# Feed-forward phase of a decoder layer: gate and up products from seven block products, gated values through memory, down product by token quarters

## The chip, the core and the metric

One core of one Trainium2 chip runs the whole layer as one program. The metric is the device time of one execution in microseconds (us). The change touches the last phase of the program only, the feed-forward part.

## The reference

The layer takes x (1 x 2048 x 1024, float32), mixes tokens with two kinds of sparse attention, and ends with a gated feed-forward network and a layer norm. The part that matters here:

```python
h = layer_norm(ALPHA * x + mixed @ w_out, ln1_g, ln1_b)        # 2048 x 1024
ffn = (jax.nn.silu(h @ w_gate) * (h @ w_up)) @ w_down          # w_gate, w_up: 1024 x 2816, w_down: 2816 x 1024
return layer_norm(ALPHA * h + ffn, ln2_g, ln2_b)
```

## The kernel before

The program is a row of phases with a barrier between them: projection, compression, attention, mixing (which writes h and its transpose h_t to memory) and `ffn_phase`. Every float32 product is made as three products of values in the fp32r form: each operand is split into a high part, which ScalarE rounds (`high`), and a low part, which VectorE subtracts (`low`); TensorE then adds high x high, high x low and low x high in one PSUM bank. Each is one instruction of 128 rows, 128 columns of weights and 512 moving columns.

The 2048 tokens are taken in four groups of 512 (`over_groups`: the groups 0, 1 and 3 are written out, group 2 is the body of a loop). In each group:

- **Gate and up** (`gate_up`). For each of the 22 blocks of 128 hidden columns (`f`) SyncE loads 128 columns of `w_gate` and of `w_up` (1024 x 128, 512 KB each) into `raw[0]` and `raw[1]`; ScalarE and VectorE split them into `w_hi` and `w_lo`; TensorE makes 8 x 3 products for gate and 8 x 3 for up, each in one bank. ScalarE makes silu of gate, VectorE multiplies it by up (`prod`), and the product is split again into `g_hi` and `g_lo`, which hold all 22 blocks on chip.
- **Down** (`for d in range(2 * DOWN)`). The 1024 output columns are taken in two halves of 512; in each half 11 steps bring two blocks of `w_down` rows (512 KB), and each step makes 2 blocks x 4 token tiles x 3 = 24 products into the four banks `acc[0..3]`. At the end of a half VectorE adds ALPHA x h from `y` (`after`, line 2280), and the next half may overwrite a bank only after that. The x operand of the next group is loaded between steps (`X_AFTER`).
- **Norm.** VectorE takes the moments, GpSimd the root of the variance, ScalarE normalizes, GpSimd multiplies by the gain and adds the offset (lines 2118 and 2121). For groups 0 to 2 this lies in the gate and up stage of the next group.

The order on every engine is the order of the program; engines wait for each other by counting semaphores. The two slots of `raw`, `w_hi` and `w_lo` are used in turn: a slot is loaded again after its low part is made, and split again after the product that read it (`used`). SyncE issues every transfer of the phase, in order.

Of the kernel before, what the change touches and what calls it, by code (L numbers as in the profile page):

```python
# [1940 lines left out]
GROUP = 512  # L1941
N_GROUPS = SEQ // GROUP
FT = FFN // P
DOWN = FT // 2


def ffn_phase(nc, h, h_t, w_gate, w_up, w_down, ln_g, ln_b, out):
# [4 lines left out]

    NB = GROUP // P
    HALF = D_MODEL // 2
    W_PER = 2 * FT + 2 * DOWN
    NX = KT * GROUP // D_MODEL
    X_AFTER = {2: 0, 6: 1, 13: 2, 17: 3}
    S_PER = W_PER + NX

    def raw_of_down(d, last):  # L1960

        return d if last else d + sum(1 for k in X_AFTER if k < d)

    with ExitStack() as ctx:  # L1964
# [6 lines left out]
        def psum(name, cols):  # L1971
            return ctx.enter_context(nc.psum_tensor(name, [P, cols], F32))

        raw = sb("f_raw", [P, 2, D_MODEL])
        w_hi = sb("f_w_hi", [P, 2, D_MODEL], F32R)
        w_lo = sb("f_w_lo", [P, 2, D_MODEL], F32R)
        x_hi = sb("f_x_hi", [P, KT, GROUP], F32R)
        x_lo = sb("f_x_lo", [P, KT, GROUP], F32R)
        silu = sb("f_silu", [P, 2, GROUP])
        prod = sb("f_prod", [P, 2, GROUP])  # L1980
        g_hi = sb("f_g_hi", [P, FT, GROUP], F32R)
        g_lo = sb("f_g_lo", [P, FT, GROUP], F32R)
        y = sb("f_y", [P, NB, D_MODEL])
        g_b = sb("f_ln_g", [P, D_MODEL])
        b_b = sb("f_ln_b", [P, D_MODEL])
# [8 lines left out]
        gate_ps = [psum(f"f_gate{b}", GROUP) for b in range(2)]  # L1994
        up_ps = [psum(f"f_up{b}", GROUP) for b in range(2)]
        acc = [psum(f"f_acc{b}", HALF) for b in range(NB)]

        small_ld = sem("f_small_ld")
        raw_ld = [sem(f"f_raw_ld{b}") for b in range(2)]
        y_ld = sem("f_y_ld")  # L2000
        hi_done = sem("f_hi_done")
        lo_done = sem("f_lo_done")
        used = sem("f_used")
        silu_done = sem("f_silu_done")
        prod_done = sem("f_prod_done")
        g_hi_done = sem("f_g_hi_done")
        g_lo_done = sem("f_g_lo_done")
# [12 lines left out]
        gate_cols = w_gate.rearrange("(k p) n -> p k n", p=P)  # L2020
        up_cols = w_up.rearrange("(k p) n -> p k n", p=P)
        down_rows = w_down.rearrange("(f p) n -> p f n", p=P)
        xt_rows = h_t.rearrange("(k p) n -> p k n", p=P)
        h_rows = h.rearrange("(g t p) n -> g p t n", p=P, t=NB)
        out_rows = out.rearrange("(g t p) n -> g p t n", p=P, t=NB)

        def over_groups(eng, body):

            body(0, True, False)
            body(1, False, False)  # L2030
            with eng.Fori(2, N_GROUPS - 1) as g:
                body(g, False, False)
            body(N_GROUPS - 1, False, True)

        @block.sync
        def _(sp):
            def load(s, parity, src, shape=None):

                if not isinstance(s, int) or s >= 2:
                    sp.wait_ge(lo_done, s - 1)  # L2040
                dst = raw[:, parity]
                if shape:
                    dst = dst.rearrange("p (a n) -> p a n", a=shape)
                sp.dma_start(dst, src).then_inc(raw_ld[parity], 16)

            def load_x(s, parity, g, n):
                load(s, parity, xt_rows[:, 2 * n:2 * n + 2, bass.ds(g * GROUP, GROUP)], 2)

            for dst, src in ((g_b, ln_g.broadcast_to([P, D_MODEL])), (b_b, ln_b.broadcast_to([P, D_MODEL]))):
                sp.dma_start(dst[:, :], src).then_inc(small_ld, 16)  # L2050
            for n in range(NX):
                load_x(n, n % 2, 0, n)

            def store(g):

                sp.wait_ge(y_done, NB * (g + 1))
                sp.dma_start(out_rows[bass.ds(g, 1), :, :, :].rearrange("o p t n -> (o p) t n"), y[:, :, :]).then_inc(y_out, 16)

            def body(g, first, last):
                s0 = NX + g * S_PER  # L2060
                with sp.Fori(0, FT) as f:
                    for m, cols in enumerate((gate_cols, up_cols)):
                        load(s0 + 2 * f + m, m, cols[:, :, bass.ds(f * P, P)], KT)

                if not first:
                    store(g - 1)
                    sp.wait_ge(y_out, 16 * g)
                sp.dma_start(y[:, :, :], h_rows[bass.ds(g, 1), :, :, :].rearrange("o p t n -> (o p) t n")).then_inc(y_ld, 16)
                for d in range(2 * DOWN):
                    s = raw_of_down(d, last)  # L2070
                    half, b = divmod(d, DOWN)
                    load(s0 + 2 * FT + s, s % 2, down_rows[:, 2 * b:2 * b + 2, half * HALF:(half + 1) * HALF], 2)
                    if d in X_AFTER and not last:
                        load_x(s0 + 2 * FT + s + 1, (s + 1) % 2, g + 1, X_AFTER[d])

            over_groups(sp, body)
            for t in range(NB):
                sp.wait_ge(y_done, NB * (N_GROUPS - 1) + t + 1)
                sp.dma_start(out_rows[N_GROUPS - 1, :, t, :], y[:, t]).then_inc(y_out, 16)
            sp.wait_ge(y_out, 16 * (N_GROUPS - 1 + NB))  # L2080

        def down_splits(split, split_x, g, last, after):

            for d in range(2 * DOWN):
                e = d + 2
                if e - 1 in X_AFTER and not last:
                    split_x(NX + g * S_PER + 2 * FT + raw_of_down(e, last) - 1, (raw_of_down(e, last) - 1) % 2, X_AFTER[e - 1], g)
                if e < 2 * DOWN:
                    split(NX + g * S_PER + 2 * FT + raw_of_down(e, last), raw_of_down(e, last) % 2, g * W_PER + 2 * FT + e, e % 2)
                elif not last:  # L2090
                    m = e - 2 * DOWN
                    split(NX + (g + 1) * S_PER + m, m, (g + 1) * W_PER + m, m)
                after(d)

        def raw_landed(eng, s, parity):
            eng.wait_ge(raw_ld[parity], (s - parity + 2) * 8)

        @block.gpsimd
        def _(pool):
            for c, value in ((power, -0.5), (eps, LN_EPS), (minus, -1.0)):  # L2100
                pool.memset(c[:, :], value).then_inc(fixed_set, 1)
            pool.wait_ge(fixed_set, 3)
            pool.wait_ge(small_ld, 32)

            def body(g, first, last):
                n0 = g * NB
                for t in range(NB):
                    pool.wait_ge(aggr_done, n0 + t + 1)
                    pool.tensor_tensor(rstd[:, t:t + 1], aggr[:, t, 1:2], eps[:, :], ALU.add).then_inc(rstd_done, 1)  # L2109
                    pool.tensor_tensor(nmr[:, t:t + 1], aggr[:, t, 0:1], minus[:, :], ALU.mult).then_inc(rstd_done, 1)  # L2110
                    pool.wait_ge(rstd_done, 4 * (n0 + t) + 2)
                    pool.tensor_tensor(rstd[:, t:t + 1], rstd[:, t:t + 1], power[:, :], ALU.pow).then_inc(rstd_done, 1)
                    pool.wait_ge(rstd_done, 4 * (n0 + t) + 3)
                    pool.tensor_tensor(nmr[:, t:t + 1], nmr[:, t:t + 1], rstd[:, t:t + 1], ALU.mult).then_inc(rstd_done, 1)
                for t in range(NB):
                    pool.wait_ge(normed, n0 + t + 1)
                    if not last:
                        pool.tensor_tensor(y[:, t], y[:, t], g_b[:, :], ALU.mult).then_inc(gained, 1)

                    pool.wait_ge(gained, n0 + t + 1)  # L2120
                    pool.tensor_tensor(y[:, t], y[:, t], b_b[:, :], ALU.add).then_inc(y_done, 1)  # L2121

            over_groups(pool, body)

        @block.tensor
        def _(pe):
            def product(out, a, w, start, stop):
                return pe.matmul(out, a, w, start=start, stop=stop)  # L2128

            def body(g, first, last):  # L2130
                s0, w0 = NX + g * S_PER, g * W_PER

                def gate_up(f, q, wait_bank):
                    for m, ps in enumerate((gate_ps, up_ps)):
                        pe.wait_ge(lo_done, s0 + 2 * f + m + 1)
                        if wait_bank:

                            pe.wait_ge(prod_done, g * FT + f - 1)
# [219 lines left out]
```

## Time and profile before

| what | value |
|---|---|
| time of three runs | 4007.77, 4009.16 and 4015.93 us, median 4009.16 |
| profiled execution, its own time | 4008.02 us |
| its span, first to last instruction | 4006.0 us |
| mean granted TensorE clock | 0.945 |
| TensorE busy | 3669.9 us, 92% of the span |
| VectorE, ScalarE, GpSimd busy | 1838.5, 1650.0 and 765.1 us |
| moved by DMA | 273.15 MB, 68 GB/s |

The durations below come from the one profiled execution. Its own time is 2.0 us above its span. A matmul row shows a matmul from issue to its last result; several are in the pipe at once, so the distance between the starts of two of them is what one of them costs in a dense stretch, and not its duration. PEclk is the granted clock as a share of full speed.

### The profile page before, as it was taken

To read this page: it belongs to the slowest core of one execution; us is meant where nothing else is said; L and a number is where in the kernel's file an instruction comes from. 1 tells how busy PE (TensorE), PEld (TensorE's weight loads), DVE (VectorE), ACT (ScalarE), POOL (GpSimd) and SP (SyncE) were. 2 spreads that over 40 slices of the span, in tenths; PEclk is the share of its full clock that TensorE was granted. 3 is DMA by queue.
4 is the path that set the end of the run, shared out by engine and by line. 5 is a ranking of instruction groups with operands and counts; after the bars stand their busy time and mean duration, and the time that the engine had idled before them with its cause. 6 is when DMAs were issued, how large, how long until landed. Compare 5 with 4: busy or idle time off the path is not lost. (4 is left out here: it accounts for less than half of the span.)

```text
span 4006.0 us, 56003 instructions
## 1 busy us (share of the span) xinstructions
PE 3669.9 (92%) x19448; PEld 3110.9 (78%) x19448; DVE 1838.5 (46%) x4296; ACT 1650.0 (41%) x2690; POOL 765.1 (19%) x1650
## 2 busy tenths in 40 slices
PE   6999768989898999999999697999999999999997
PEld 5999647877777788888778585788788788878885
DVE  4222145666666666776664343333343243324323
ACT  2000024667666677677765332232232233223321
POOL 0000023454343333332321132000020020002001
PEclk9999768999999999999889898999999999999998
DMA  4221220000000000000000354333333433433342
GB/s 144 74 69 62 67 50 26 24 16 22 16 9 16 15 16 13 10 7 10 4 6 6 124 158 147 105 94 129 103 94 112 135 100 94 142 109 96 94 136 74
DMA packets 302064, 273.15 MB, mean 68 GB/s; under 512 B 32544, under 2 KB 249760, under 8 KB 299680
## 3 DMA queue, kind: packets, MB, share of 16 engines
q1 hardware_dynamic: 300368, 268.31, 21.8%
q10 hardware_dynamic: 1488, 2.20, 0.2%
q8 instruction: 114, 1.87, 0.2%
q14 instruction: 94, 0.77, 0.1%
HBM read 218.57 MB, written 51.90 MB: 68 GB/s over the span
## 5 line engine op out<-in xcount | busy, mean ns | idle before, releaser
L2224 DVE TENSOR_TENSOR f_w_lo<-f_raw,f_w_hi 128x1024 fp32r<-128x1024 f32 x264 | 337.3, 1278 | 883.7 <-ACT f_w_hi L2176 883.7
L2176 ACT ACTIVATE f_w_hi<-f_raw 128x1024 fp32r<-128x1024 f32 x264 | 279.9, 1060 | 882.6 <-PE f_acc L2128 337.2
L1285 ACT ACTIVATE a_p_t<-a_ps_st 128x512 f32<-128x512 f32 x716 | 438.0, 614 | 371.3 <-PE a_ps_st L1175 191.7
L1292 ACT ACTIVATE a_junk_a<-a_index,a_tk 128x384 bf16<-128x384 f32 (+13 forms) x336 | 445.0, 1325 | 110.3 <-DVE a_halves L1402 55.6
L1201 PEld LDWEIGHTS a_ps_o<-a_vsl,a_p_t 128*128 128x128 f32 x2176 | 315.5, 209 | 26.4 <-DVE a_fin L1499 3.4
L2128 PE MATMUL f_gate<-f_x_hi,f_w_hi 128*128 128x512 f32 x704 | 275.1, 391 | 30.2 <-DVE f_w_lo L2224 30.2
L1201 PE MATMUL a_ps_o<-a_vsl,a_p_t 128*128 128x65 f32 x2176 | 298.2, 284 | 2.1 <-DVE a_fin L1499 2.1
L1201 PEld LDWEIGHTS a_ps_o<-a_dv,a_p_t 128*128 128x128 f32 x2176 | 290.0, 194 | 9.0
L2128 PE MATMUL f_acc<-f_w_hi,f_g_hi 128*128 128x512 f32 x704 | 278.6, 396 | 16.4 <-DVE f_y L2280 12.6
L2128 PE MATMUL f_acc<-f_w_lo,f_g_hi 128*128 128x512 f32 x704 | 277.2, 394 | 0.0
L2128 PE MATMUL f_acc<-f_w_hi,f_g_lo 128*128 128x512 f32 x704 | 277.0, 393 | 0.0
L2128 PE MATMUL f_gate<-f_x_lo,f_w_hi 128*128 128x512 f32 x704 | 274.6, 390 | 0.0
L2128 PE MATMUL f_gate<-f_x_hi,f_w_lo 128*128 128x512 f32 x704 | 274.6, 390 | 0.0
L2109 POOL TENSOR_TENSOR f_rstd<-f_aggr,f_eps 128x1 f32<-128x1 f32 x16 | 6.5, 406 | 1402.1 <-DVE f_aggr L2254 1402.1
L1201 PE MATMUL a_ps_o<-a_dv,a_p_t 128*128 128x65 f32 x2176 | 274.0, 269 | 0.0
L2128 PE MATMUL f_up<-f_x_hi,f_w_hi 128*128 128x512 f32 x704 | 273.9, 389 | 0.0
L2128 PE MATMUL f_up<-f_x_lo,f_w_hi 128*128 128x512 f32 x704 | 273.9, 389 | 0.0
L2128 PE MATMUL f_up<-f_x_hi,f_w_lo 128*128 128x512 f32 x704 | 273.9, 389 | 0.0
L188 PE MATMUL p_acc<-pw_hi,px_hi 128*128 128x448 f32 x640 | 238.5, 373 | 34.2 <-DVE pw_lo L267 33.9
L188 PE MATMUL p_acc<-pw_lo,px_hi 128*128 128x448 f32 x640 | 237.3, 371 | 0.0
L188 PE MATMUL p_acc<-pw_hi,px_lo 128*128 128x448 f32 x640 | 237.3, 371 | 0.0
L1382 DVE SCALAR_TENSOR_TENSOR a_index<-a_relu,a_iw,a_index 128x512 f32<-128x512 f32 (+3 forms) x266 | 179.7, 716 | 99.6 <-ACT a_relu L1279 96.9
(268 smaller groups left out, 7556.7 us busy)
## 6 DMA issues: line engine op xcount, KB each, us to landing
f_raw<-in_w_gate SPq DMA_DIRECT2D x88, 512.0 KB, 3.8
f_raw<-in_w_up SPq DMA_DIRECT2D x88, 512.0 KB, 3.8
f_raw<-in_w_down SPq DMA_DIRECT2D x88, 512.0 KB, 3.3
z_scratch<-p_z SPq DMA_DIRECT2D x16, 1120.0 KB, 5.2
pw_raw<-in_w_in SPq DMA_DIRECT2D x16, 560.0 KB, 3.8
px_raw<-in_x_t SPq DMA_DIRECT2D x16, 512.0 KB, 6.4
o_scratch<-a_oacc SPq DMA_DIRECT2D x32, 256.0 KB, 2.1
m_o_in<-o_scratch SPq DMA_DIRECT2D x16, 512.0 KB, 4.5
```

What stands on the lines that cost most here:

```text
L188: mm = pe.matmul(acc[c][:, 0:CH], xs[:, u, k], ws[:, k, c * CH:(c + 1) * CH], start=(k == 0 and n == 0), stop=last)
L1201: mm = pe.matmul(ps_o[n % 2][:, h * cols:(h + 1) * cols], p_t[:, s % PT_RING, h * P:(h + 1) * P], v, start=(j == 0 and h == 0), stop=(j == ...
L1285: act.activation(p_t[:, s % PT_RING, :], ps_st[s % ST_BANKS][:, :], ACT.Exp, scale=SCALE).then_inc(exp_done, 1)
L1292: act.activation(junk_a[:, 0:w], index[t % 2][:, 0:w], ACT.Sign, bias=thr, scale=-1.0, accum_out=cnt).then_inc(counted, 1)
L1382: dve.scalar_tensor_tensor(dst, relu[:, r % RELU_RING, 0:w], weight, dst, ALU.mult, ALU.add).then_inc(index_done, 1)
L2109: pool.tensor_tensor(rstd[:, t:t + 1], aggr[:, t, 1:2], eps[:, :], ALU.add).then_inc(rstd_done, 1)
L2128: return pe.matmul(out, a, w, start=start, stop=stop)
L2176: act.activation(w_hi[:, slot], raw[:, parity], ACT.Copy).then_inc(hi_done, 1)
L2224: dve.tensor_tensor(w_lo[:, slot], raw[:, parity], w_hi[:, slot].bitcast(F32), ALU.subtract).then_inc(lo_done, 1)
```

## The change

The tokens are taken in two groups of 1024, each as two parts of 512. For a pair of hidden blocks (256 columns of `w_gate` or `w_up`: a *set*, 22 sets in a group) the product of the 256 x 1024 weights by the 1024 x 1024 tokens is seen as a 2 x 2 block product: the inner dimension in halves of 512, the hidden columns in two blocks of 128, the tokens in two parts. Instead of eight block products, seven are made (`block_product`, 4 x 3 matmuls each), of sums of blocks:

- GpSimd forms four sums of weight blocks for each set (`sums`, 128 x 512 each) and, once per group, eight sums of token blocks of 128 x 1024 (`turn_x`).
- ScalarE and VectorE split seven weight operands of 128 x 512 per set (`high`, `low`) where it was two of 128 x 1024 per block and group, and seven operands of the tokens per group (`high_x`, `low_x`).
- VectorE joins the seven products into four results with seven additions from PSUM (`summed`), after ScalarE has copied the first one out (`first_kept`); per pair of sets there are four silu and four multiplications (`gated`) of 128 x 512.

The gated values no longer stay on chip: they go to the scratch tensor `g_all` (`store_g`, 1 MB per pair) and come back in the down stage. This stage takes a quarter of the tokens (512) at a time; each of its 22 steps loads one block of `w_down` rows over all 1024 columns (512 KB) and one block of gated values (256 KB), splits both, and makes 4 token tiles x 2 halves x 3 = 24 products into eight banks. Every loop is written out. The buffers of the tokens at the start are borrowed from `gs`, `y` and the norm's parameters; the latter are loaded later.

The core of the diff:

```diff
...
-GROUP = 512
+GROUP = 1024
 N_GROUPS = SEQ // GROUP
+PART = GROUP // 2
 FT = FFN // P
-DOWN = FT // 2
...
+HALF = D_MODEL // 2
+ORDER = 7
+SUMS_AT = ((), (0,), (1,), (2, 3), (4,), (5,), (6,))
+FREED = (0, 1, 2, 4, 5, 6)
...
+U_PER = ORDER * SETS + 2 * FT
+L_PER = ORDER * SETS + 4 * FT
+X_AT = {0: {10: 0, 13: 1, 14: 2, 15: 3, 16: 4, 17: 5, 18: 6}, 1: {8: 0, 11: 1, 12: 2, 13: 3, 14: 4, 15: 5, 16: 6}}
...
+        def product_bank(G, n, j):
+            return bank[(2 * G + ORDER * n + j) % 8]
+        def acc(G, a):
+            return bank[(2 * G + ORDER * SETS - 8 + a) % 8]
...
+            def load_set(G, n):
+                b, m = divmod(n, 2)
+                if G or b:
+                    sp.wait_ge(lo_done, l_set(G, n - 1) if b else l_set(G, 0) - 2 * (1 - m))
+                for half in range(2):
+                    sp.dma_start(w_half(m, half), w_cols[m][:, 4 * half:4 * half + 4, 2 * b * P:2 * (b + 1) * P]).then_inc(raw_ld[2 * m + half], 16)
+            def load_step(G, F):
+                hq, f = divmod(F, FT)
+                u = F % 2
+                sp.wait_ge(lo_done, l_set(G, SETS - 1 + F) if F < 2 else l_step(G, F - 2) + 1)
+                sp.dma_start(raw[:, 2 * u], down_rows[:, f, :]).then_inc(raw_ld[2 * u], 16)
+                if F >= 2:
+                    sp.wait_ge(lo_done, l_step(G, F - 2) + 2)
+                b = f // 2
...
+                cols = slice(G * GROUP + hq * PART, G * GROUP + (hq + 1) * PART)
+                sp.dma_start(raw[:, 2 * u + 1, 0:PART], g_rows[:, f, cols]).then_inc(raw_ld[2 * u + 1], 16)
+            def store_g(G, b):
+                sp.wait_ge(g_done, 4 * (G * PAIRS + b + 1))
+                sp.dma_start(g_rows[:, 2 * b:2 * b + 2, G * GROUP:(G + 1) * GROUP],
+                             gs[:, :, :].rearrange("p (f t) n -> p f (t n)", f=2)).then_inc(g_out[b % 2], 16)
...
+            load_set(0, 0)
+            for block_no in (0, 1, 3):
+                load_x(0, None, block_no)
+            load_set(0, 1)
+            sp.wait_ge(x_lo_done, 6)
+            load_x(0, None, 2)
...
+                            sp.wait_ge(g_out[1], 16 * 5)
+                        else:
+                            sp.wait_ge(x_lo_done, 3 * ORDER)
+                        for block_no in (0, 1, 3, 2):
+                            load_x(1, r, block_no)
+                    if F == FT + 12:
+                        store_y(2 * G)
+                    if F == FT + 14:
+                        load_y(2 * G + 1)
+                if G == 0:
+                    load_set(1, 0)
+                    load_set(1, 1)
...
+                m = n % 2
+                N = G * SETS + n
+                for k in only:
+                    number = 4 * N
+                    if k == 3:
+                        pool.wait_ge(lo_done, l_set(G, n) + 2)
+                    elif N:
+                        pool.wait_ge(lo_done, (l_set(G, n - 1) if n else l_set(G - 1, SETS - 1)) + (4, 3, 7)[k])
+                    if k == 0:
+                        for half in range(2):
+                            pool.wait_ge(raw_ld[2 * m + half], raw_value(G, n))
...
+                        op = pool.tensor_tensor(s_block(1), s_block(0), a_block(m, 0, 0), ALU.subtract)
+                    else:
+                        pool.wait_ge(s_done, number + 3)
+                        op = pool.tensor_tensor(s_block(1), a_block(m, 0, 1), s_block(1), ALU.subtract)
+                    op.then_inc(s_done, 1)
...
+            def turn_x(G, r, n):
+                b11, b12, b21, b22, t2 = x_blocks(G, r)
+                ld = 16 * (2 if G == 0 else 3 + r)
+                if n == 0:
+                    pool.wait_ge(x_ld[1], ld)
+                    pool.wait_ge(x_lo_done, x_number(G, r, 0) + 1)
...
+                else:
+                    pool.wait_ge(x_ld[2], ld)
+                    pool.wait_ge(x_lo_done, x_number(G, r, 1) + 1)
+                    op = pool.tensor_tensor(t2, b21, t2, ALU.subtract)
...
+                for n in range(SETS):
+                    if n + 1 < SETS:
+                        sums(G, n + 1)
+                    if G and 1 <= n <= 4:
+                        root(2 * G - 1, n - 1)
+                    if G and 3 <= n <= 6:
+                        gains(2 * G - 1, n - 3, False)
+                if G == 0:
...
+            def block_product(G, n, j):
+                b, m = divmod(n, 2)
+                N, B = G * SETS + n, G * PAIRS + b
+                pe.wait_ge(lo_done, l_set(G, n) + j + 1)
+                if n == 0:
+                    pe.wait_ge(x_lo_done, x_upto(G, j))
+                p = ORDER * n + j
+                if p >= 8:
+                    if j == 0:
+                        pe.wait_ge(sum_done, ORDER * (N - 1))
+                    elif j == 1:
+                        pe.wait_ge(first_kept, N)
+                    else:
+                        pe.wait_ge(sum_done, ORDER * (N - 1) + FREED[j - 1])
+                elif G:
+                    pe.wait_ge(added, 8 * (2 * G - 1) + p + 1)
+                out = product_bank(G, n, j)
+                for k in range(4):
+                    for i, (w, x) in enumerate(((w_hi, x_hi), (w_hi, x_lo), (w_lo, x_hi))):
+                        mm = pe.matmul(out[:, :], w[:, j, k * P:(k + 1) * P], x[:, j, k], start=(k == 0 and i == 0),
+                                       stop=(k == 3 and i == 2))
+                mm.then_inc(used, 1)
...
+                pe.wait_ge(lo_done, l_step(G, F) + 2)
+                for t in range(NB):
+                    cols = slice(t * P, (t + 1) * P)
...
+                            mm = pe.matmul(acc(G, a)[:, :], x[:, s + 2, cols], w[:, s + half, :], start=(f == 0 and i == 0), stop=(f == FT - 1 and i == 2))
+                    if f == FT - 1 and t < NB - 1:
+                        mm.then_inc(acc_full, 1)
...
+            def high(G, n, j):
+                m = n % 2
+                N = G * SETS + n
+                if n:
+                    act.wait_ge(used, u_set(G, n - 1) + j + 1)
+                elif G:
+                    act.wait_ge(used, u_set(G, 0) - (1 if j < 3 else 0))
+                if j in (0, 4, 5):
+                    act.wait_ge(raw_ld[2 * m + (j > 0)], raw_value(G, n))
+                else:
+                    act.wait_ge(s_done, 4 * N + {3: 1, 2: 2, 1: 3, 6: 4}[j])
+                act.activation(slot(w_hi, j), source(m, j), ACT.Copy).then_inc(hi_done, 1)
...
+            for j in range(ORDER):
+                for r in range(2):
+                    high_x(0, r, j)
+                high(0, 0, j)
...
+                b, m = divmod(n, 2)
+                s0 = ORDER * (G * SETS + n)
+                m1, u2, u3 = uu[:, 3 * m], uu[:, 3 * m + 1], uu[:, 3 * m + 2]
+                piece = product_bank(G, n, (1, 2, 3, 3, 4, 5, 6)[k])[:, :]
+                dve.wait_ge(used, u_set(G, n) + (2, 3, 4, 4, 5, 6, 7)[k])
+                if k == 0:
...
+                elif k == 3:
+                    dve.wait_ge(sum_done, s0 + 2)
+                    if m == 0 and b:
+                        dve.wait_ge(g_out[(b - 1) % 2], 16 * (G * (6 - (b - 1) % 2) + (b - 1) // 2 + 1))
...
+            def gated(G, b, k):
+                dve.wait_ge(silu_done, 4 * (G * PAIRS + b) + k + 1)
+                dve.wait_ge(sum_done, ORDER * (G * SETS + 2 * b + 1) + 4 + k)
+                dve.tensor_tensor(gs[:, PLACE[k]], gs[:, PLACE[k]], uu[:, (0, 3, 5, 4)[k]], ALU.mult).then_inc(g_done, 1)
...
+            def add_h(q):
+                dve.wait_ge(y_ld, 16 * (q + 1))
...
-                        dve.wait_ge(aggr_done, n0 + t)
+                    if t < NB - 1:
+                        dve.wait_ge(acc_full, (NB - 1) * q + t + 1)
+                    else:
...
+                    for j in range(ORDER):
+                        for k in SUMS_AT[j]:
+                            summed(G, n, k)
+                        if n + 1 < SETS:
+                            low(G, n + 1, j)
+                        elif j in DOWN_AT:
+                            low_step(G, *DOWN_AT[j])
+                        if m and j >= 3:
+                            gated(G, b, j - 3)
+                        if G and j == 3 and n < NB:
...
+                    if hq and 1 <= f <= NB:
+                        moments(2 * G, f - 1)
+                if G == 0:
+                    for j in range(3):
+                        low(1, 0, j)
+                add_h(2 * G + 1)
+                if G == 0:
+                    for j in range(3, ORDER):
+                        low(1, 0, j)
+            q = 2 * N_GROUPS - 1
...
```

## Rows read from the trace of the kernel before

**Rows 1.** The page, part 1: busy time, share of the span, instructions of each engine.
```profile
PE 3669.9 (92%) x19448; PEld 3110.9 (78%) x19448; DVE 1838.5 (46%) x4296; ACT 1650.0 (41%) x2690; POOL 765.1 (19%) x1650
```
**Rows 2.** Windows (busy time by engine, PEclk, DMA share, GB/s), a stretch of the phase.
```profile
3200.00:3600.00 400.00, 394.21 (x1725) 325.23 (x1724) 138.84 (x145) 109.22 (x125) 29.37 (x24) 0.99 0.36 111
```
**Rows 3.** Timeline, start and end of the phase; brackets: idle before, and who ended it.
```profile
2487.63 0.10 POOL L2101 MEMSET f_power<- 128x1 f32 x1 [6.36 <-POOLq L1595]
...
2494.59 1.06 ACT L2183 ACTIVATE f_x_hi<-f_raw 128x1024 fp32r<-128x1024 f32 x1 [10.67 <-DMA f_raw<-ht_scratch]
2495.87 1.06 ACT L2183 ACTIVATE f_x_hi<-f_raw 128x1024 fp32r<-128x1024 f32 x1 [0.23 <-DMA f_raw<-ht_scratch]
...
2509.27 0.79 PE L2128 MATMUL f_gate<-f_x_hi,f_w_hi 128*128 128x512 f32 x1 [25.98 <-DVE f_w_lo L2224]
...
2510.28 0.63 PE L2128 MATMUL f_gate<-f_x_hi,f_w_lo 128*128 128x512 f32 x1
2510.71 0.63 PE L2128 MATMUL f_gate<-f_x_hi,f_w_hi 128*128 128x512 f32 x1
...
3970.13 0.39 PE L2128 MATMUL f_acc<-f_w_hi,f_g_hi 128*128 128x512 f32 x1
...
3979.42 0.39 PE L2128 MATMUL f_acc<-f_w_hi,f_g_lo 128*128 128x512 f32 x1
```
**Rows 4.** Timeline of TensorE where one product's bank ends and the next begins.
```profile
2532.75 0.39 PE L2128 MATMUL f_up<-f_x_hi,f_w_lo 128*128 128x512 f32 x1
2532.98 0.39 PE L2128 MATMUL f_gate<-f_x_hi,f_w_hi 128*128 128x512 f32 x1
```
**Rows 5.** Waits of TensorE after 2500 us: total, times, longest.
```profile
PE f_gate L2128 <- DVE f_w_lo L2224: 30.2, 4, 26.0
PE f_acc L2128 <- DVE f_y L2280: 12.6, 4, 3.2
PE f_acc L2128 <- DVE f_w_lo L2224: 3.8, 3, 1.3
```
**Rows 6.** Windows, a stretch with one of the waits for f_y in it.
```profile
3545.00:3555.00 10.00, 6.84 (x18) 5.32 (x18) 3.62 (x5) 1.06 (x1) 0.00 (x0) 0.66 0.15 53
```
**Rows 7.** Groups of instructions from 2485 us to the end: count, busy, mean ns, idle before.
```profile
L2224 DVE TENSOR_TENSOR f_w_lo<-f_raw,f_w_hi 128x1024 fp32r<-128x1024 f32 x264 | 337.3, 1278 | 883.7 <-ACT f_w_hi L2176 883.7
L2176 ACT ACTIVATE f_w_hi<-f_raw 128x1024 fp32r<-128x1024 f32 x264 | 279.9, 1060 | 882.6 <-PE f_acc L2128 337.2 <-PE f_up L2128 326.7 <-PE f_gate L2128 151.4
L2128 PE MATMUL f_gate<-f_x_hi,f_w_hi 128*128 128x512 f32 x704 | 275.1, 391 | 30.2 <-DVE f_w_lo L2224 30.2
...
L2267 DVE TENSOR_TENSOR f_prod<-f_silu,f_up 128x512 f32<-128x512 f32 x88 | 59.8, 680 | 0.0
...
L2118 POOL TENSOR_TENSOR f_y<-f_y,f_ln_g 128x1024 f32<-128x1024 f32 x12 | 37.7, 3139 | 4.6 <-ACT f_y L2193 4.6
...
L2228 DVE TENSOR_TENSOR f_x_lo<-f_raw,f_x_hi 128x1024 fp32r<-128x1024 f32 x16 | 19.5, 1220 | 21.2 <-ACT f_x_hi L2183 21.2
```
**Rows 8.** Timeline of GpSimd and VectorE where both work at once.
```profile
2896.68 0.19 POOL L2114 TENSOR_TENSOR f_nmr<-f_nmr,f_rstd 128x1 f32<-128x1 f32 x1
2897.34 1.06 POOL L2109 TENSOR_TENSOR f_rstd<-f_aggr,f_eps 128x1 f32<-128x1 f32 x1 [0.48 <-DVE f_aggr L2254]
...
2902.01 2.40 POOL L2118 TENSOR_TENSOR f_y<-f_y,f_ln_g 128x1024 f32<-128x1024 f32 x1 [1.54 <-ACT f_y L2193]
...
2897.18 2.35 DVE L2224 TENSOR_TENSOR f_w_lo<-f_raw,f_w_hi 128x1024 fp32r<-128x1024 f32 x2
...
3992.75 10.21 POOL L2121 TENSOR_TENSOR f_y<-f_y,f_ln_b 128x1024 f32<-128x1024 f32 x4
...
3994.10 2.07 DVE L2296 TENSOR_TENSOR f_y<-f_y,f_ln_g 128x1024 f32<-128x1024 f32 x1 [1.35 <-ACT f_y L2193]
```
**Rows 9.** DMA issues after 2500 us: KB each, median us to landing.
```profile
f_raw<-in_w_down SPq DMA_DIRECT2D x88, 512.0 KB, 3.3
f_y<-h_scratch SPq DMA_DIRECT2D x4, 2048.0 KB, 7.8
```

More of the change, by code:

```diff
@@ new lines, in u_step, with l_step, raw_value, w_half @@
+        def u_step(G, F):
+            return u_set(G, SETS) + F
+        def l_step(G, F):
+            return l_set(G, SETS) + 2 * F
+        def raw_value(G, n, F=None):
+            return 16 * (G * 3 * PAIRS + (n // 2 if F is None else PAIRS + F // 2) + 1)
+        def w_half(m, half):
+            return raw[:, 2 * m + half].rearrange("p (k n) -> p k n", k=4)
+        def a_block(m, row, half):
+            return w_half(m, half)[:, :, row * P:(row + 1) * P]
+        def s_block(n):
+            return st[:, n].rearrange("p (k n) -> p k n", k=4)
@@ L2049, in _ @@
[L2049 to L2074, printed above, removed]
@@ L2076, in _ @@
-            over_groups(sp, body)
-            for t in range(NB):
[L2078 to L2093, printed above, removed]
@@ L2169, in _ @@
+            for G in range(N_GROUPS):
+                for n in range(SETS):
+                    for j in range(ORDER):
+                        block_product(G, n, j)
+                for F in range(2 * FT):
+                    down_step(G, F)
         @block.scalar
         def _(act):
-            def high(s, parity, w, slot):
-                raw_landed(act, s, parity)
-                if not isinstance(w, int) or w >= 2:
-                    act.wait_ge(used, w - 1)
-                act.activation(w_hi[:, slot], raw[:, parity], ACT.Copy).then_inc(hi_done, 1)
@@ L2195, in body @@
-            def body(g, first, last):
-                s0, w0 = NX + g * S_PER, g * W_PER
-                def tile(f, q, wait):
-                    high(s0 + 2 * f + 2, 0, w0 + 2 * f + 2, 0)
-                    act.wait_ge(used, w0 + 2 * f + 1)
-                    if wait:
-                        act.wait_ge(prod_done, g * FT + f - 1)
-                    act.activation(silu[:, q], gate_ps[q][:, :], ACT.Silu).then_inc(silu_done, 1)
-                    high(s0 + 2 * f + 3, 1, w0 + 2 * f + 3, 1)
-                    act.wait_ge(prod_done, g * FT + f + 1)
-                    act.activation(g_hi[:, bass.ds(f, 1)].rearrange("p o n -> p (o n)"), prod[:, q], ACT.Copy).then_inc(g_hi_done, 1)
-                tile(0, 0, not first)
-                tile(1, 1, not first)
-                if not first:
-                    norm(g - 1)
-                with act.Fori(1, FT // 2) as f2:
-                    for q in range(2):
-                        tile(2 * f2 + q, q, True)
-                down_splits(high, high_x, g, last, lambda d: None)
@@ L2220, in _ @@
+            for t in range(NB):
+                norm(2 * N_GROUPS - 1, t)
         @block.vector
         def _(dve):
[L2222 to L2229 removed]
@@ L2299, in layer @@
+            q = 2 * N_GROUPS - 1
+            for t in range(NB):
+                moments(q, t)
+            for t in range(NB):
+                dve.wait_ge(normed, q * NB + t + 1)
+                dve.wait_ge(gained, q * NB + t)
+                dve.tensor_tensor(y[:, t], y[:, t], g_b, ALU.mult).then_inc(gained, 1)
 def layer(nc, ap, out):
```

471 lines of the change are left out of this document (296 added, 175 removed).

## The prediction, made before the changed kernel ran

> **What bounds the kernel now.** I read the page first, then windows of the last phase, then TensorE's waits and its timeline there. On the page TensorE is busy 92% of the span and no other engine reaches half [rows 1]; in a window inside the phase it is busy 394.2 of 400 us at a granted clock of 0.99 [rows 2]. The reader is to see that VectorE (139), ScalarE (109) and GpSimd (29 us) wait for it there, not it for them. The phase begins at 2487.6 (call it T) and its first matmul at 2509.27; the last one begins at 3979.42 and takes its share of 0.23, so TensorE's stretch ends near 3979.7, and 26.3 us of adding, norm and store follow to 4006.0 [rows 3]. In the stretch, 1470.4 us, lie nine forms of matmul with 704 each [rows 7], 6336 in all. At full clock one costs 0.2267 us: from the one at 3970.13 to the last one lie 41 steps in 9.29 us [rows 3]; a change of bank costs nothing on top, 2532.75 to 2532.98 [rows 4]. That is 1436.2 us. Waits take 30.2 - 26.0 + 12.6 + 3.8 = 20.6 [rows 5]. The 13.6 left is half clock: the first matmuls stand 0.43 apart [rows 3], and around a wait of 3.2 us the granted clock is 0.66 [rows 6]. What counts for the change is therefore the number of matmuls, the waits, and the two ends.
>
> **Matmuls.** Gate and up: 2 groups x 22 sets x 84 = 3696 where it was 4224; down: 2 x 44 x 24 = 2112, unchanged. 5808 in all, 528 fewer: 528 x 0.2267 = -119.7. A set lasts 84 x 0.2267 = 19.04 us, a block product 2.72, a down step 5.44.
>
> **Does anything else need more than 19.04 per set?** VectorE: seven low parts of 128 x 512 (half of 1.28, say 0.65), seven additions from PSUM (0.68), and per pair four multiplications (0.68) [rows 7]: 9.3, or 12.0 in a set of up. ScalarE: seven roundings of 0.53, a copy and two silu on average, some 5.5. GpSimd: four sums at half of 2.40 [rows 8], 4.8. VectorE and GpSimd do disturb each other: a GpSimd operation of 0.19 takes 1.06 when it begins beside two subtractions with both inputs on chip, and VectorE's multiplication of 1024 takes 2.07 beside a row of GpSimd's where such an instruction is otherwise 1.2 [rows 8, 7]. If they took strict turns, with even the PSUM additions in the line, a set of up would need 12.0 + 4.8 = 16.8, still under 19.04. Latency is no problem either: a weight slot is free after its product of the set before and is needed seven products later, 16.3 us against some 2 for rounding and subtracting; a bank is needed again eight products on. The store of gated values (1 MB) is issued about 3 us into a set, behind 1 MB of weights, and must land before `summed` k = 3 some 11 us in; 2 MB take 7.8 us [rows 9], so VectorE may wait 1 to 3 us there, inside that margin. I take the steady gate and up stage as dense, 0 lost.
>
> The Trainium skill, page "SBUF — State Buffer", section "Who interferes with whom", says that a VectorE instruction with two SBUF inputs and a GpSimd instruction that reads SBUF exclude each other for a whole instruction. The rows of 1.06 and 2.07 fit that. By it the start below is the serial one, T+61; without it T+51.
>
> **The start.** Before: first matmul at T+21.7; its set's worth of work (19.04, and some 2 for half clock) would be over at T+42.7. After: SyncE asks for 1 MB of weights, then three token blocks of 1 MB. Before, four transfers of 512 KB had landed at T+7 to T+8.3 [rows 3], and 2048 KB take 7.8 [rows 9], so a megabyte each 3.9: weights T+5, block 0 T+8.5, block 1 T+12.5, block 3 T+16. GpSimd must then work off 8 token sums of 2.40 and 4 weight sums of 1.2 = 24 us, in an order in which product 1 waits for the first four token sums and three weight sums. Undisturbed: product 0 at T+13.5; product 1 after 12.5 + 4 x 2.4 + 2 x 1.2 = T+24.5, plus rounding and subtracting, T+26; product 2 T+33; products 3 to 6 follow each split of two token halves and a weight (2 x 1.23 + 0.65 = 3.1), with block 2 asked for only after product 2's operands, landing near T+37; product 6 at T+48, set 0 over at T+51. With strict turns: VectorE's 14 x 1.22 + 7 x 0.65 = 21.6 and GpSimd's 24 lie in one line, product 1 at T+31, block 2 landing at T+42.5, product 6 at T+57, and the matmuls partly at 0.43: set 0 over at T+61 to T+65. The rows favour turns, but not every operation collides: I take T+58, 15.3 later than before. Set 1 finds its operands ready (GpSimd and ScalarE are by then ahead of it).
>
> **Down stage.** Removed: 12.6 at the halves [rows 5] with the half clock behind them, since a quarter's end now frees pairs of banks in turn (`acc_full`) while TensorE still fills the others: VectorE adds two banks (2 x 0.68) per 1.36 us of matmuls. Also gone are most of the 3.8 and of the 4.2 (30.2 less the first 26.0) at group borders [rows 5]: one border is left instead of three. Added per step: the split of gated values. After step F-2 frees the slot: 0.2 + 1.06 (high) + 1.23 (low) + 0.65 (low of g), about 3.2 of 5.44; the slack is 2.2. GpSimd's big operations fall here: per group eight of the norm, and in group 0 eight token sums, 24 x 2.4 us over some 15 steps. One of them can hold a subtraction back by up to 2.4, two of them by 4.8. Cost: 0 if they never meet, 15 x 2 = 30 if each such step loses 2; I take 10. The transfers per step, 768 KB, are some 3 us of a window of 7.5 between issue and use; six bursts of 2 MB (y, tokens) lie in between, of 7.8 each [rows 9]; the like cost 1.3 before [rows 5]: 0 to 8, I take 2. Border between groups and into the down stage: 2. Sum of new stalls 14, between 2 and 38.
>
> **The tail.** The last adds need only two banks after the last matmul instead of four: two adds of 0.68 fewer, some 0.4 lost again on the last bank's wait: 26.3 becomes 25.3.
>
> **Sum.** From T: 58 + (5808 - 84) x 0.2267 (1297.4) + 14 + 25.3 = 1394.7, where it was 1518.4. That is -123.7: span 3882.3, own time 3884.3 by the same 2.0; the median of the runs is 1.1 above the profiled execution's own time, so 3885. Seen the other way: -119.7 matmuls, -20.6 waits, -11.6 of half clock (2 stay with the start), +15.3 start, +14 stalls, -1.0 tail.
>
> **Bounds.** Low: 48 + 1297.4 + 2 + 25 gives 3863. High: 65 + 1297.4 + 38 + 26.3 gives 3917.
>
> **Rivals.**
> (a) *The down stage becomes bound by latency.* If the gated values land late or the chain of 3.2 us is really above 5.44, each of 88 steps grows. At 1 us per step: +88, 3973. For it: two splits in a row on two engines, a read just behind a write. Against: 2.2 us of slack in a plain step, and DMA at about a third of its time even now [rows 2].
> (b) *The gate and up stage is bound by VectorE and GpSimd.* With 16.8 of 19.04 in strict turns, own waits between dependent additions of 0.2 us for each of 11 could pass 19.04 in sets of up; sets of gate have slack to give back. At 1 us per set over 44: +44, about 3929.
> (c) *Slower than before.* One wait of TensorE in each set, at the bank that `summed` must free or at the weight sum of `sums` k = 3. The price is not the wait alone: a wait of 3.2 us brings the granted clock to 0.66 over 10 us [rows 6], about 2 us more, while waits of 1.3 did not show it. The gain is 124 over 44 sets, so it decides from 2.8 us per set in all; with a wait of 3.2 and 2 for the clock: 44 x 5.2 = 229, at 4114. Against it stand margins of 14 us at every such wait; it needs an order that I misread.
> (d) *The matmuls don't get fewer in time:* a wait each 12 matmuls instead of each 24 costs a gap. At 0.2 us for each of 308 block products: +62, 3947. Rows 4 show no gap at a bank border with its waits met.
>
> **The numbers.** Forecast 0.74, (a) 0.09, (b) 0.09, (c) 0.03, (d) 0.03; 0.02 for less than the low bound. The range 3862 to 3918 holds the forecast's bounds. A measurement of this kernel can tell 0.2%, 8 us, from no change. Faster 0.95, same 0.01, slower 0.04.
>
> **What the changed profile would show.** 3696 and 2112 matmuls 0.2267 apart; in a window inside the gate and up stage TensorE busy all of it, with `gated` of one pair 38.1 us after the pair before; product 1 of set 0 at T+26 to T+31 and set 1 beginning at T+51 to T+65; no wait for f_y over 1 us in the down stage, but waits of 1 to 3 us for f_w_lo where GpSimd multiplies y. The prediction is wrong if sets are further apart than 19.04, if steps are further apart than 5.44 without GpSimd's work beside them, or if half clock outlasts set 0.

## The result, and the profile after

The changed kernel takes 3884.56 us in the median of four runs (3878.05 to 3890.73), the kernel before 4008.47 in four: ratio 0.9687, interval 0.9663 to 0.9711. The profiled execution's own time is 3879.3, its span 3877.5.

The page of the changed kernel, parts 1 and 2, with the lines that answer to [rows 1]:

```profile
PE 3548.9 (92%) x18920; PEld 3010.5 (78%) x18920; DVE 2122.2 (55%) x4748; ACT 1694.9 (44%) x2878; POOL 1063.5 (27%) x1842
...
PEclk9999777999999999999899989799999999999998
```

528 matmuls fewer, as the diff says, at 121 us less TensorE time; VectorE has 284 us more work and GpSimd 298. Windows in the gate and up stage (first and third row; the first reaches 13 us into the down stage) and in the down stage (second and fourth), to be read beside [rows 2], which covers both stages of the kernel before. Below them is a window of the kernel before that lies in gate and up alone:

```profile
2560.00:2960.00 400.00, 400.00 (x1767) 331.31 (x1766) 241.18 (x334) 127.78 (x204) 110.10 (x76) 1.00 0.28 94
3000.00:3100.00 100.00, 98.82 (x436) 81.39 (x435) 59.95 (x67) 38.68 (x46) 27.18 (x24) 1.00 0.49 163
3200.00:3600.00 400.00, 400.00 (x1766) 331.35 (x1765) 254.34 (x352) 135.95 (x217) 142.46 (x105) 1.00 0.28 94
3700.00:3840.00 140.00, 137.55 (x603) 112.57 (x602) 71.32 (x74) 44.05 (x54) 29.05 (x24) 1.00 0.50 171
...
2550.00:2800.00 250.00, 250.00 (x1105) 207.01 (x1104) 83.16 (x86) 71.59 (x87) 0.00 (x0) 1.00 0.36 109
```

In gate and up TensorE is busy all of the 400 us at full clock, although VectorE went from 33% to 60% there in the first window of each kernel, and GpSimd, which had nothing to do in that one, to 28%. Only the down stage has gaps. TensorE's waits after 2490 us, against [rows 5]:

```profile
PE f_ps L2308 <- DVE f_w_lo L2429: 38.5, 4, 20.2
PE f_ps L2328 <- DVE f_w_lo L2439: 4.8, 8, 1.2
```

The first row is the start of the phase: all four of its waits lie before 2537. The second is all that the rest of the phase waits. The timeline of TensorE, start of the phase and its last matmul, against [rows 3]:

```profile
2503.37 0.80 PE L2308 MATMUL f_ps<-f_x_hi,f_w_hi 128*128 128x512 f32 x1 [20.21 <-DVE f_w_lo L2429]
...
2517.49 0.80 PE L2308 MATMUL f_ps<-f_x_hi,f_w_hi 128*128 128x512 f32 x1 [9.47 <-DVE f_w_lo L2429]
...
2523.64 0.50 PE L2308 MATMUL f_ps<-f_x_hi,f_w_hi 128*128 128x512 f32 x1 [1.73 <-DVE f_w_lo L2429]
...
2536.65 0.80 PE L2308 MATMUL f_ps<-f_x_hi,f_w_hi 128*128 128x512 f32 x1 [7.13 <-DVE f_w_lo L2429]
...
3851.95 0.39 PE L2328 MATMUL f_ps<-f_w_hi,f_w_lo 128*128 128x512 f32 x1
```

With T = 2487.5 (GpSimd's first memset of the phase) the products begin at T+15.9 (product 0), T+30.0 (product 1), T+36.1 (product 2, with 3 behind it) and T+49.1 (product 4, with 5 and 6 behind it); set 1 follows without a gap at 2547.0, T+59.5. So the phase after splits as: 59.5 to the end of set 0; 2547.0 to 3852.2 = 1305.2 for 5724 matmuls, of which 1297.4 at 0.2267; 25.3 of tail. Sum 1390.0, where it was 1518.4.

### The profile page after: what moved, and what is told of

It is laid out like the page before. It is cut to its first block and busy times, and to the rows that moved or that the text cites. A ratio compares the mean times of both kernels' runs of the same rounds, so it can differ in the third digit from the quotient of the medians.

```text
span 3877.5 us, 54790 instructions
## 1 busy us (share of the span) xinstructions
PE 3548.9 (92%) x18920; PEld 3010.5 (78%) x18920; DVE 2122.2 (55%) x4748; ACT 1694.9 (44%) x2878; POOL 1063.5 (27%) x1842
## 3 DMA queue, kind: packets, MB, share of 16 engines
q8 instruction: 137, 2.24, 0.2%
## 5 line engine op out<-in xcount | busy, mean ns | idle before, releaser
L2308 PE MATMUL f_ps<-f_x_hi,f_w_hi 128*128 128x512 f32 x1232 | 482.3, 391 | 38.5 <-DVE f_w_lo L2429 38.5
L2308 PE MATMUL f_ps<-f_x_lo,f_w_hi 128*128 128x512 f32 x1232 | 481.2, 391 | 0.0
L2308 PE MATMUL f_ps<-f_x_hi,f_w_lo 128*128 128x512 f32 x1232 | 481.0, 390 | 0.0
L2308 PEld LDWEIGHTS f_ps<-f_x_hi,f_w_hi 128*128 128x128 f32 x1232 | 232.6, 189 | 89.1 <-DVE f_w_lo L2429 40.5
L2328 PE MATMUL f_ps<-f_w_hi 128*128 128x512 f32 x704 | 275.0, 391 | 4.9 <-DVE f_w_lo L2439 4.8
L2328 PE MATMUL f_ps<-f_w_hi,f_w_lo 128*128 128x512 f32 x704 | 274.0, 389 | 0.0
L2328 PE MATMUL f_ps<-f_w_lo,f_w_hi 128*128 128x512 f32 x704 | 274.0, 389 | 0.0
L2308 PEld LDWEIGHTS f_ps<-f_x_lo,f_w_hi 128*128 128x128 f32 x1232 | 232.8, 189 | 48.0
L2308 PEld LDWEIGHTS f_ps<-f_x_hi,f_w_lo 128*128 128x128 f32 x1232 | 232.5, 189 | 48.3
L2435 DVE TENSOR_TENSOR f_w_lo<-f_raw,f_w_hi 128x1024 fp32r<-128x1024 f32 x88 | 121.4, 1379 | 240.6 <-ACT f_w_hi L2363 240.6
```

The lines of the kernel that those rows point to most:

```text
L2308: mm = pe.matmul(out[:, :], w[:, j, k * P:(k + 1) * P], x[:, j, k], start=(k == 0 and i == 0), stop=(k == 3 and i == 2))
L2328: mm = pe.matmul(acc(G, a)[:, :], x[:, s + 2, cols], w[:, s + half, :], start=(f == 0 and i == 0), stop=(f == FT - 1 and i == 2))
L2435: dve.tensor_tensor(w_lo[:, s:s + 2], raw[:, 2 * (F % 2)].rearrange("p (a n) -> p a n", a=2), w_hi[:, s:s + 2].bitcast(F32), ALU.subtract) ...
```

## The experiments

All are edits of the changed kernel. Single runs of the changed kernel differ by up to 13 us (of the kernel before, in the thirteen taken beside the first experiment, by 18), and its profiles by what lies ahead of the changed phase (last experiment). So I compare the length of the phase, from GpSimd's first memset in it to the end of the span, in one profile each. The changed kernel gave 1390.0 and, run again, 1389.4; "longer" and "shorter" are against their mean, 1389.7.

**An eighth product.**

```diff
-                for k in range(4):
+                for again in range(2 if j == 0 else 1):
+                    for k in range(4):
...
```

> In every set the first block product is made twice in its bank, so a set has eight block products (96 matmuls) and everything else stays as in the changed kernel; the result is the same. Theory (gate and up stage bound by TensorE alone, the gain is the 528 matmuls): 528 x 0.2267 = +119.7 us, span 3877.5 + 119.7 = 3997. Rival (the stage is partly bound by VectorE and GpSimd, or the block products wait for sums): part of the extra product fills waits, and the span grows by less than 100, to under 3978.

Measured: span 3999.6, phase 1506.3, longer by 116.6. Ten runs have the median 4000.56, ratio to the kernel before 0.9972 (0.9959 to 0.9984). Of the 119.7 the first set's share, 2.7, falls into the wait between product 0 and product 1, where it costs nothing; 117.0 is left to be expected. ScalarE's copies of the first product show the distance of the sets (19.04 + 2.72 = 21.76):

```profile
2710.09 0.60 ACT L2401 ACTIVATE f_u<-f_ps 128x512 f32<-128x512 f32 x1 [4.81 <-PE f_ps L2309]
...
2731.85 0.60 ACT L2401 ACTIVATE f_u<-f_ps 128x512 f32<-128x512 f32 x1 [4.08 <-PE f_ps L2309]
```

The same copies in the changed kernel:

```profile
2702.24 0.60 ACT L2400 ACTIVATE f_u<-f_ps 128x512 f32<-128x512 f32 x1 [1.36 <-PE f_ps L2308]
...
2721.28 0.60 ACT L2400 ACTIVATE f_u<-f_ps 128x512 f32<-128x512 f32 x1 [2.09 <-PE f_ps L2308]
```

Each product counts in full: gate and up is bound by TensorE alone. The run also prices the rest of the change: with as many matmuls as before, the new order of the phase takes 1506.3 where the old took 1518.4, 12.1 less.

**Two of three matmuls**, to find the next bound.

```diff
-                    for i, (w, x) in enumerate(((w_hi, x_hi), (w_hi, x_lo), (w_lo, x_hi))):
+                    for i, (w, x) in enumerate(((w_hi, x_hi), (w_hi, x_lo), (w_lo, x_hi))[0:2 if N else 3]):
...
```

> Left out: from the second set on, the low part of the weights is still made but not multiplied, so a set of gate or up has 56 matmuls instead of 84 (12.7 us instead of 19.04) and the result is less exact. It shows how near the next bound lies. TensorE alone: 43 x 28 x 0.2267 = -273, span 3605. VectorE and GpSimd in strict turns, 18 + 14 VectorE instructions at 0.60 and 8 of GpSimd at 1.2 per pair of sets = 28.8 us where TensorE has 25.4: 22 pairs x 9.3 = -205, span 3673. The store of the gated values as the bound (2 MB to be moved before the fourth addition of the next pair): waits of VectorE for that store in the trace, and a span between the two or above.

Measured: span 3688.5, phase 1197.2: 192.5 shorter, not 273, and near the 205 of strict turns. ScalarE's copy of the first product of every second set, so one pair apart, and VectorE at the fourth addition; below them VectorE and GpSimd side by side:

```profile
2701.67 0.58 ACT L2400 ACTIVATE f_u<-f_ps 128x512 f32<-128x512 f32 x1
...
2730.52 0.58 ACT L2400 ACTIVATE f_u<-f_ps 128x512 f32<-128x512 f32 x1
...
2724.46 0.69 DVE L2464 TENSOR_TENSOR f_gs<-f_u,f_ps 128x512 f32<-128x512 f32 x1 [2.87 <-DMA g_scratch<-f_gs]
...
2704.75 0.67 DVE L2457 TENSOR_TENSOR f_u<-f_u,f_ps 128x512 f32<-128x512 f32 x1
2705.35 1.40 DVE L2429 TENSOR_TENSOR f_w_lo<-f_st,f_w_hi 128x512 fp32r<-128x512 f32 x1
...
2704.90 1.30 POOL L2209 TENSOR_TENSOR f_st<-f_raw,f_st 128x512 f32<-128x512 f32 x1 [1.83 <-DVE f_w_lo L2429]
```

A pair takes 28.8 us where TensorE needs 25.4. VectorE is without a gap but for one wait of 2.9 for the store of the gated values, which comes just where the prediction looked for it, and one of 1.1 for ScalarE's rounding. In the changed kernel the pair takes 38.1, so the margin to the next bound is some 9 us in such a pair. It is not the same everywhere: in the second group the pairs beside the norm of the quarter before, with GpSimd's gain and offset in them, take up to 34.6, which leaves 3.5. That the estimate for strict turns, 28.8, was met is chance. It has no share for the store's wait (without it a pair would take some 26, an estimate by subtraction), and it had the additions from PSUM in the turns. They do not take part: in the last three rows such an addition takes 0.67 beside GpSimd's sum, while the subtraction behind it, with both inputs on chip, takes 1.40 instead of 0.68.

**Block 2 early.** It gets a place in `uu`, free until the first sum:

```diff
-                return (gs[:, ks], late, late, y[:, 2 + r, :]
+                return (gs[:, ks], late, uu[:, ks], y[:, 2 + r, :]
...
-            for block_no in (0, 1, 3):
+            for block_no in (0, 1, 3, 2):
                 load_x(0, None, block_no)
             load_set(0, 1)
-            sp.wait_ge(x_lo_done, 6)
-            load_x(0, None, 2)
```

> The third token block of the start (inner half 2, tokens 1) gets a place of its own in the buffer of the sums and is loaded at once, instead of after the operands of product 2. Theory (the start is a chain of transfers and of turns of GpSimd and VectorE, in which the late block costs the wait of 7.1 us before product 4): set 0 ends 5 to 7 us earlier, span 3871 to 3873. Rival (the late block only hides work of GpSimd and VectorE that must be done anyway): under 2 us.

Measured: span 3881.0 with the phase beginning late, at 2494.7; phase 1386.3, shorter by 3.4. Neither theory, but between the two. The wait before product 4 falls from 7.1 to 1.7:

```profile
2541.96 0.50 PE L2306 MATMUL f_ps<-f_x_hi,f_w_hi 128*128 128x512 f32 x1 [1.71 <-DVE f_w_lo L2427]
```

But the last token sums now start on GpSimd while VectorE makes the operands of products 2 and 3 (T+33.3 instead of T+40.7), and these products come 1.1 and 3.5 later. The late transfer had covered that much of the turns.

**Token sums on VectorE.**

```diff
-            for r in range(2):
-                turn_x(0, r, 0)
...
+                for n in {0: (0, 1), 1: (2,), 3: (3,)}.get(j, ()):
+                    for r in range(2):
+                        turn_x(0, r, n)
```

(The removed lines stood in GpSimd's program, the added ones stand in VectorE's, between `low_x` and `low`.)

> The eight token sums of 128 x 1024 at the start are made by VectorE instead of GpSimd, in the places where they fit its order; the four weight sums stay on GpSimd. Theory (GpSimd and VectorE exclude each other, and GpSimd needs 2.4 for what VectorE does in 1.2): the common line gets 8 x 1.2 = 9.6 us shorter, set 0 ends 8 to 11 earlier, span 3867 to 3870. Rival (VectorE is the engine that sets the start, GpSimd is beside it): VectorE gets 9.8 us more work, set 0 ends at the same time or up to 10 us later, span 3877 to 3888.

Measured: span 3869.9, phase 1378.3, shorter by 11.4. VectorE has eight subtractions more to do at the start, 10.1 us in the trace, and the start is shorter: the two engines form one line there. The timeline of GpSimd and VectorE in the changed kernel shows the line itself:

```profile
2498.21 2.36 DVE L2443 TENSOR_TENSOR f_x_lo<-f_gs,f_x_hi 128x1024 fp32r<-128x1024 f32 x2 [19.49 <-ACT f_x_hi L2375]
2500.49 2.83 DVE L2429 TENSOR_TENSOR f_w_lo<-f_raw,f_w_hi 128x512 fp32r<-128x512 f32 x1
2509.00 4.46 DVE L2443 TENSOR_TENSOR f_x_lo<-f_lnp,f_x_hi 128x1024 fp32r<-128x1024 f32 x2 [5.68 <-ACT f_x_hi L2375]
...
2492.79 1.26 POOL L2201 TENSOR_TENSOR f_st<-f_raw 128x512 f32<-128x512 f32 x1 [5.11 <-DMA f_raw<-in_w_gate]
...
2510.14 2.24 POOL L2203 TENSOR_TENSOR f_st<-f_raw 128x512 f32<-128x512 f32 x1
```

Two VectorE subtractions take 2.36 alone and 4.46 beside GpSimd; a weight sum takes 1.26 alone and 2.24 beside VectorE; a subtraction of 0.68 takes 2.83.

**No gain and offset in the down stage.**

```diff
+                    cut = slice(0, 8) if q % 2 == 0 else slice(0, D_MODEL)
-                    pool.tensor_tensor(y[:, t], y[:, t], g_b, ALU.mult).then_inc(gained, 1)
+                    pool.tensor_tensor(y[:, t, cut], y[:, t, cut], g_b[:, cut], ALU.mult).then_inc(gained, 1)
...
```

> Left out: for the token quarters 0 and 2 GpSimd multiplies and adds only 8 of 1024 columns in the norm, so the output of these quarters is not the layer's. Theory (the eight waits of TensorE in the down stage, 4.8 us in all and 7 with what follows each, come from GpSimd's operations of 2.4 us that take turns with the two subtractions of a step): all eight waits vanish, span 3870 to 3871. Rival (the moments and the norm on VectorE and ScalarE, or the transfers, make these steps late): waits of the same size stay.

Measured: all eight waits gone, phase 1381.7, shorter by 8.0. In the changed kernel one such step looks like this (GpSimd, VectorE and TensorE):

```profile
3091.29 3.25 POOL L2249 TENSOR_TENSOR f_y<-f_y,f_lnp 128x1024 f32<-128x1024 f32 x1
...
3092.22 2.87 DVE L2439 TENSOR_TENSOR f_w_lo<-f_raw,f_w_hi 128x512 fp32r<-128x512 f32 x1
...
3095.08 3.34 DVE L2435 TENSOR_TENSOR f_w_lo<-f_raw,f_w_hi 128x1024 fp32r<-128x1024 f32 x1
...
3095.14 0.50 PE L2328 MATMUL f_ps<-f_w_hi 128*128 128x512 f32 x1 [1.18 <-DVE f_w_lo L2439]
...
3101.28 0.50 PE L2328 MATMUL f_ps<-f_w_hi 128*128 128x512 f32 x1 [0.41 <-DVE f_w_lo L2439]
```

The subtraction of 0.68 waits out an operation of GpSimd, and so does the one of 1.23 before it (2.65 to 3.34 in these steps). In each of the two groups of tokens four steps in a row are late, the first by 1.3, the next three by 0.71 each: they stand 6.15 apart instead of 5.44. The token sums hold VectorE back as well, but only one of the two subtractions of a step:

```profile
3114.59 1.21 DVE L2435 TENSOR_TENSOR f_w_lo<-f_raw,f_w_hi 128x1024 fp32r<-128x1024 f32 x1
3115.72 2.88 DVE L2439 TENSOR_TENSOR f_w_lo<-f_raw,f_w_hi 128x512 fp32r<-128x512 f32 x1
```

No wait of TensorE follows there. One held subtraction costs 2.2, which is just the slack that the prediction gave a step; two cost 3.6 in the first late step (2.65 - 1.23 and 2.87 - 0.68), 1.4 more than the slack.

**GpSimd paced.** One large operation per step, begun when both subtractions are done; the tokens' second batch, the store and the load of y move back by some steps:

```diff
+                    if q % 2 == 0:
+                        pool.wait_ge(lo_done, l_step(q // 2, F) + 2)
                     pool.tensor_tensor(y[:, t], y[:, t], g_b, ALU.mult).then_inc(gained, 1)
...
```

> In the down stage GpSimd starts each of its big operations (gain, offset, and the second batch of token sums) only when both subtractions of a step are done, one operation per step, so that it works while VectorE is idle; the store and load of y and the token operands move back by some steps. All work is kept. Theory (it is the turns that cost): no waits over 0.3 us in the down stage, span 3870 to 3872. Rival (GpSimd's work costs wherever it lies, or the moved 2 MB transfers make a step late): waits of 0.4 to 1.2 us remain or come at other steps, span 3875 or more.

Measured: no wait of TensorE in the whole down stage with all work kept, phase 1381.3, shorter by 8.4. The span is 3876.7, outside the expected 3870 to 3872, because the phase began late, at 2495.4; counted in the phase, 5.5 to 7.5 less was expected and 8.4 less came. GpSimd and VectorE there:

```profile
3098.46 2.39 POOL L2250 TENSOR_TENSOR f_y<-f_y,f_lnp 128x1024 f32<-128x1024 f32 x1 [2.79 <-DVE f_w_lo L2445]
...
3101.91 1.23 DVE L2441 TENSOR_TENSOR f_w_lo<-f_raw,f_w_hi 128x1024 fp32r<-128x1024 f32 x1 [3.61 <-ACT f_w_hi L2369]
...
3103.05 0.68 DVE L2445 TENSOR_TENSOR f_w_lo<-f_raw,f_w_hi 128x512 fp32r<-128x512 f32 x1
...
3103.81 2.39 POOL L2254 TENSOR_TENSOR f_y<-f_y,f_lnp 128x1024 f32<-128x1024 f32 x1 [2.96 <-DVE f_w_lo L2445]
```

**The three edits together.**

> All three edits together: token block 2 loaded at once, the eight token sums at the start on VectorE, GpSimd paced in the down stage. All work is kept. Theory: start 11 to 15 us shorter, down stage 7 shorter, span 3855 to 3860. Rival (they remove the same wait, or the early block delays the others): the sum of the parts is not reached, span 3864 or more.

Measured: 3864.68 in the median of four runs (3858.41 to 3868.43), ratio to the kernel before 0.9629 (0.9606 to 0.9652); span 3860.0, phase 1367.3, shorter by 22.4 where the parts add up to 23.2. A surprise stands in GpSimd's timeline:

```profile
2501.01 1.26 POOL L2204 TENSOR_TENSOR f_st<-f_st,f_raw 128x512 f32<-128x512 f32 x1
2515.02 17.10 POOL L2207 TENSOR_TENSOR f_st<-f_raw,f_st 128x512 f32<-128x512 f32 x1 [12.74 <-DVE f_w_lo L2425]
```

VectorE's row from 2514.85 to 2530.97 has no gap and two inputs on chip in every instruction, and the weight sum ends only after it, at 2532.12. Product 6 waited 2.2 for it.

**The fourth weight sum of the first set on VectorE as well.**

```diff
+                    dve.wait_ge(s_done, 3)
+                    dve.tensor_tensor(s_block(1), a_block(0, 0, 1), s_block(1), ALU.subtract).then_inc(s_done, 1)
...
```

> The version with an early block 2, token sums on VectorE and paced GpSimd, and in addition the fourth weight sum of the very first set on VectorE. In the trace of that version this sum, 1.26 us of work, took 17.10 us on GpSimd beside a dense row of VectorE instructions, and product 6 waited for it. Theory (GpSimd is shut out for as long as VectorE's row is dense): product 6 starts about 2 us earlier, the phase lasts 1365 instead of 1367.3 us. Rival (VectorE's row is itself the limit): no change, or 0.6 us more.

Measured: 3859.01 in the median of four (3853.99 to 3864.5), ratio 0.9631 (0.9615 to 0.9647); phase 1366.0, shorter by 1.3 than without it, and product 6 no longer waits (product 4 waits 1.4 instead of 0.6, for VectorE's added work). The next sum, the first of set 1, is now the one shut out, for 11.96 us; TensorE does not wait for it. This is the shortest phase of all, though its ratio can't be told from that of the version before it. Of the two medians only the ratios compare: the kernel before took 4015.78 beside the one and 4006.61 beside the other.

**Gated values not moved.**

```diff
-                sp.dma_start(raw[:, 2 * u + 1, 0:PART], g_rows[:, f, cols])
+                sp.dma_start(raw[:, 2 * u + 1, 0:8], g_rows[:, f, G * GROUP:G * GROUP + 8])
...
```

> The changed kernel, but of each store and each load of gated values only 8 columns are moved (left out: nearly all gated values, so the output is not the layer's); the number of transfers, the splits and the products stay. Theory (the way through memory lies beside other work and costs nothing): the phase lasts 1390 us as before, within 1. Rival (the loads make steps of the down stage late, or the stores hold VectorE up): the phase gets shorter by more than 2, and some of the eight waits of the down stage go.

Measured: phase 1389.2 (1389.4 and 1390.0 with the traffic), the same eight waits. The gated values' way through memory costs nothing here.

**The changed kernel again.**

> The changed kernel again, unchanged. Its four runs so far lie at 3878, 3879, 3890 and 3891 us. If that is a difference of single executions in the phases ahead of the change, a profile near 3889 shows the feed-forward phase 1390 us long as before and the 11 us elsewhere; if it lies in the new phase (its transfers, the start), the phase is some 1400 us long.

Measured: 3882.57 in the median (3880.19 to 3890.25). The profile's span is 3883.1, 5.6 above the first profile's, and the phase begins 6.2 later, at 2493.7, and lasts 1389.4. Over the eleven profiles of the changed kernel and its edits the phase begins between 2486.3 and 2495.4. So the differences between profiles of one kernel lie ahead of the changed phase. Of the 6.2 between these two, 2.1 are there when the compression begins, near 440 us, and 5.8 at 640 us, early in attention; from there to the changed phase it stays about 6.2. What makes them is open, and no execution at 3890 was itself profiled.

## Why the prediction was right

- **Matmuls, -119.7.** Right, and shown by the eighth product (116.6 of the 117.0 that can show).
- **A dense gate and up stage, 0 lost.** Right: no wait in 43 sets, 19.04 apart. The margin was real (28.8 of 38.1 in most pairs), and the store of the gated values is part of what comes next. In the changed kernel VectorE waited for that store twice, 0.8 at most, where the prediction allowed 1 to 3 per pair.
- **The start, T+58.** T+59.5. The line of turns was the cause, as the token sums on VectorE show: -11.4 where turns gave 8 to 11. Product 1 came at T+30.0 (T+26 and T+31 were the two cases), block 2 landed near T+40.6 (T+37 and T+42.5), product 6 began at T+56.8 (T+48 and T+57). So the start follows the case of strict turns closely, and the discount down to T+58, "not every operation collides", was 1.5 too much. The exclusion that the Trainium skill states (page "SBUF — State Buffer", section "Who interferes with whom") is what the rows of 2.24, 2.83 and 4.46 show. The T+61 worked out with turns was nearer than the T+51 without them.
- **Down stage, 14.** The step whose size was off: 7.8, of which 4.8 are the eight waits (0.4 to 1.2 each, where the signs named 1 to 3). Mechanism and place were right (GpSimd's gain and offset beside the two subtractions; no waits without them). But only four steps per group were late, not some 15: the token sums on GpSimd lie in other steps and hold up one subtraction there, which the slack of 2.2 takes. The prediction had the two cases (2.4 for one held subtraction, 4.8 for two) and the slack, and did not set them against each other. The transfers, for which I took 2, show no wait: the gated values' were left out without effect, and no wait of ScalarE for a load of weights or gated values stands in the trace of the down stage. What the bursts of 2 MB cost was not tried by itself.
- **Waits and half clock of before, -20.6 and -11.6.** Gone: after set 0 every window of 10 us that is full of matmuls or holds one of the eight waits shows a granted clock of 1.00.
- **Tail, 25.3.** 25.3 (no experiment bears on it).
- **Sum.** Phase 1394.7 predicted, 1390.0 measured: 1.5 more at the start, 6.2 less in the down stage. Own time of the profiled execution 3884.3 against 3879.3. That the median of the runs is within 0.5 of 3885 is luck: two of the four runs lay near 3890.
- **The rivals.** (a) fell with the traffic left out and with 5.44 per step; (b) with the eighth product; (d) with the sets 19.04 apart, which is 84 times 0.2267 with nothing for the seven changes of product (the eighth product does not test it, as it waits for nothing); (c), a wait in each set, did not occur.

## What to carry to other kernels

Seven block products for eight pay in full where TensorE is the only bound, and the additions they need are free as long as the engine that makes them keeps a margin in every set; run the stage with fewer matmuls to see how much is left. Count GpSimd and VectorE as one line wherever both work on operands that all lie on chip, above all in a start where nothing else is running (VectorE's additions with one input in PSUM are not in that line): there it can be better to give the busier engine the work. In a loop with a short period, set what GpSimd can hold back in one step against the slack of that step, and start GpSimd's large operations on a signal that VectorE's part of the step is done.

## What the hardware showed unexpectedly

Turns are not assured. In most places GpSimd and VectorE alternated: 3.25 and 2.87 us for operations of 2.4 and 0.68. Beside a VectorE row without any gap one GpSimd operation of 1.26 us took 17.10, and another one 11.96, while the first of these two sums took 2.21 in the version with only the token sums moved. In both cases of a shut-out the operation ended 1.2 us after the row did (2532.12 after 2530.97, and 2530.96 after 2529.80), about its own length: as if it had waited for the whole row and then run. What decides between the two is open. The moment of the start is not it: the sum of 2.21 began 0.16 us behind a VectorE subtraction, the one of 17.10 began 0.17 behind the same subtraction.
